# Column sums, folds and score matmuls of a hybrid decoder step: partial work moved from TensorE to VectorE, transposes for folds, page loads reordered

## What is computed

```python
(s_m, a_m, g_m, s_f, a_f, g_f) = silu(c) @ W_ada + b_ada
h = RMSNorm(x) * (1 + a_m) + s_m
p = h @ W_in
A = MLA(p)         # latent attention; the samples attend to paged cache rows
B = ShortConv(p); C = ChunkGMLP(p)
x = x + g_m * W_o(sig(gA)*A + sig(gB)*B + sig(gC)*C)
x = x + g_f * MoE(RMSNorm(x) * (1 + a_f) + s_f)    # 64 experts, top 8, 1 shared
```

## Time and profile before

| | |
|---|---|
| median of 3 runs | 1101.2 us |
| the profiled execution | 1101.79 us |
| its span (first to last instruction) | 1100.1 us |
| TensorE busy | 1052.6 us (96%) |
| VectorE busy | 387.0 us (35%) |
| ScalarE busy | 226.8 us (21%) |
| mean granted TensorE clock | 0.985 |

### The profile page before, as it was taken

One profiled execution on the slowest core, in us unless ns is written; L12 is line 12 of the kernel. 1 busy time (PEld: TensorE's weight loads), 2 busy tenths in 40 slices (PEclk: granted clock), 3 DMA queues, 4 the chain that ended last, 5 costly groups with the idle time before them and its releaser, 6 DMA issues.

```text
span 1100.1 us, 14510 instructions
## 1 busy us (share of the span) xinstructions
PE 1052.6 (96%) x4963; PEld 606.4 (55%) x4963; DVE 387.0 (35%) x1057; ACT 226.8 (21%) x464; POOL 56.6 (5%) x80
## 2 busy tenths in 40 slices
PE   7999999888999899999899999999999999999996
PEld 3477766444444678887673444444444444444443
DVE  1403211246774111112362334334334343433334
ACT  2311222133443300000421111111111111211110
POOL 0100001000000000000010000000000000000000
PEclk9999999899999999999899999999999999999998
DMA  8974467644345672343429999999999999999971
GB/s 318 420 310 165 162 216 226 146 127 132 96 122 190 211 330 115 138 169 130 176 94 396 415 414 409 408 416 402 406 409 412 398 404 414 410 405 414 400 310 41
DMA packets 52353, 310.11 MB, mean 282 GB/s; under 512 B 8538, under 2 KB 27018, under 8 KB 30802
## 3 DMA queue, kind: packets, MB, share of 16 engines
q1 hardware_dynamic: 46018, 296.13, 69.1%
q0 software_dynamic: 6288, 13.37, 3.4%
HBM read 314.80 MB, written 2.80 MB: 289 GB/s over the span
## 4 chain that ended last, share of the span: by engine, by line
PE 86%; SPq 6%; DMA 3%; issue 3%; DVE 1%; ACT 0%; DVEq 0%; ACTq 0%
PE bank L632 48%; PE pA L632 22%; PE pB L632 6%; PE pC L632 5%; SPq L386 3%; PE bank L1153 3%; SPq L427 2%; PE bank L1143 1%; DMA adx<-in_w_ada 1%; DMA pT<-in_poolT 1%; PE bank L1173 1%; PE pD L632 0%; DVE pT L2059 0%; SPq L422 0%; PE bank L1064 0%
## 5 line engine op out<-in xcount | busy, mean ns | idle before, releaser
L632 PE MATMUL pA<-ring,qT 128*64 128x512 f32 x1024 | 226.7, 595 | 0.0
L632 PE MATMUL bank<-hT,ring 128*128 128x264 f32 (+1 forms) x864 | 199.3, 390 | 1.0 <-PE bank L632 1.0
L632 PEld LDWEIGHTS bank<-hT,ring 128*128 128x128 f32 (+1 forms) x864 | 162.9, 190 | 36.2 <-issue 8.0
L632 PEld LDWEIGHTS pA<-ring,qT 128*64 128x64 f32 x1024 | 70.8, 137 | 133.7 <-issue 133.7
L632 PE MATMUL bank<-pT,vtok 128*128 128x264 f32 x512 | 127.6, 393 | 0.9 <-ACT vtok L1561 0.9
L632 PEld LDWEIGHTS bank<-pT,vtok 128*128 128x128 f32 x512 | 92.2, 190 | 39.4 <-issue 26.9
L2059 DVE TENSOR_TENSOR pT<-pT,bank 128x264 f32<-128x264 f32 x256 | 106.8, 427 | 12.2 <-PE bank L632 9.9
L632 PE MATMUL bank<-wuk,ring 128*128 128x512 f32 x192 | 89.9, 618 | 0.0
L2067 DVE TENSOR_TENSOR oaT<-oaT,pA 128x256 f32<-128x256 f32 x32 | 13.5, 421 | 197.9 <-ACT oaT L1557 197.9
L632 PEld LDWEIGHTS bank<-wuk,ring 128*128 128x128 f32 x192 | 36.4, 197 | 47.9 <-issue 47.7
L632 PE MATMUL pB<-ring,oaT 128*64 128x512 f32 x256 | 62.0, 605 | 0.5 <-ACT oaT L1540 0.5
(11 more groups left out here) (279 smaller groups left out, 884.3 us busy)
## 6 DMA issues: line engine op xcount, KB each, us to landing
ring<-in_w_e_gu SPq DMA_DIRECT2D x64, 2048.0 KB, 10.0
ring<-in_w_e_dn SPq DMA_DIRECT2D x64, 1024.0 KB, 10.4
ring<-in_poolT SPq DMA_DIRECT2D x64, 208.0 KB, 2.7
ring<-in_w_ada SPq DMA_DIRECT2D x12, 1024.0 KB, 8.2
ring<-in_w_bg SPq DMA_DIRECT2D x4, 3072.0 KB, 10.6
ring<-in_w_mix SPq DMA_DIRECT2D x5, 2048.0 KB, 8.8
ring<-in_w_ada SPq DMA_DIRECT2D x4, 2048.0 KB, 13.2
ring<-in_poolR SPq DMA_DIRECT2D x50, 128.0 KB, 2.1
```

Of the source, the lines that this page charges most:

```text
L632: return nc.tensor.matmul(out, lhsT, rhs, start=start, stop=stop)
```

## The change

- `sumsq` becomes `colsum`: VectorE adds the tiles first (`tile_sums`, one strided TENSOR_REDUCE), and one ones-matmul adds over the partitions. This holds for norm1, cqn, kvn, vmean and vvar. In norm2 VectorE adds the squares tile by tile, and two ones-matmuls stand after the last output tile.
- `ada_fold` and `scores_fold` become four transposes against `ident`. VectorE adds over the groups (`ada_sum`, twelve of them, and a second instruction in `take_scores`). pA holds one item at a time, so a fold waits for the sum before it (`adsum`, `folded`).
- The rotary part of `scores` is four matmuls of 256 columns in four column groups.
- `qlat` is eight matmuls of 256 columns in four column groups, a copy on ScalarE and four transposes.
- On SP, `ada_item(10)` goes ahead of `pages_t(0, 1)`. 28 row pages of the second group are issued inside the sequence loop, up to five behind each `pages_t`, into space whose weights have been used; the last four follow `row_values(0)`, ahead of g0.
- On the POOL queue `ident` is loaded first, in place of `fold`; `fold2` goes.
- On VectorE the norm of the queries (`head_norm(0)`) comes ahead of `head_var("ksum", 1)`.

The diff, cut to its core:

```diff
         rowpg = [rest(0, PGE, 11) + rest(1, PGE, 11) + rest(3, H * KL + 8 * P, 10),
-                 rest(1, PGE, 11) + rest(2, QT * H * P + KT_ * H * NOPE, 7)
-                 + [qTf[:, x * KL:(x + 1) * KL] for x in range(8)] + [kTf[:, x * KL:(x + 1) * KL] for x in range(6)]]
+                 rest(2, 0, 12) + rest(2, DT * 512, 8) + [adx[:].rearrange("p a c -> p (a c)")[:, x * KL:(x + 1) * KL]
+                                                          for x in range(8)] + rest(1, PGE, 4)]
+        LATE = 4
...
             ada_item(9)
+            ada_item(10)
             pages_t(0, 1)
-            ada_item(10)
             ada_item(11)
...
-            with sp.Fori(1, NS // 2) as i:
+            for i in range(1, NS // 2):
                 for b in range(2):
                     pages_t(i, b)
+                    x = (2 * (i - 1) + b) * 5
+                    pages_r(1, x, min(x + 5, HALF - LATE))
...
             values_done(0)
+            pages_r(1, HALF - LATE, HALF)
             gates_w(0)
-            pages_r(1, 0, 18)
             gates_w(1)
-            sp.wait_ge(s["asc"], H)
-            pages_r(1, 18, HALF)
...
-            def sumsq(stage, src, nt, ready=None):
+            def colsum(stage, src, i):
                 n = BASE[stage]
                 t = enter(n)
-                for k in range(nt):
-                    last = mm(t[:, 0:NT], ones[:], src[:, k, :], k == 0, k == nt - 1)
-                last.then_inc(full[n % 4], 1)
+                pe.wait_ge(s["tilesum"], i)
+                mm(t[:, 0:NT], ones[:], src, True, True).then_inc(full[n % 4], 1)
...
             def ada_fold(x):
+                if x:
+                    pe.wait_ge(s["adsum"], x)
                 for m in range(4):
-                    last = mm(pA[:, (4 * x + m) * NC:(4 * x + m + 1) * NC], adb[:, x % 2, m * P:(m + 1) * P], fold[:],
-                              True, True)
+                    last = nc.tensor.transpose(pA[:, m * P:(m + 1) * P], adb[:, x % 2, m * P:(m + 1) * P], ident[:])
...
+            for hf in range(2):
+                for j in range(4):
+                    h = 4 * hf + j
+                    last = mm(t[32 * j:32 * j + NS, hf * KL:(hf + 1) * KL], qsg[0:NOPE, h, :], wukT[:, h, :], True, True)
+            last.then_inc(full[n % 4], 1)
+            keys(0, range(NPK // 2, NPK - 1))
...
+                    last = nc.tensor.transpose(t[:, (2 * k + hf) * P:(2 * k + hf + 1) * P],
+                                               scr[:, (2 * hf + k) * P:(2 * hf + k + 1) * P], ident[:])
...
-                for g in range(2):
-                    last = mm(t[32 * g:32 * g + 32, :], qrp[:, q, :], pgT[b][:, 4 * g:4 * g + 4, 2 * P:3 * P], False, True)
+                for k in range(KT_):
+                    for g in range(2):
+                        last = mm(t[32 * (2 * k + g):32 * (2 * k + g) + 32, k * 2 * P:(k + 1) * 2 * P], qrp[:, q, :],
+                                  pgT[b][:, 4 * g + 2 * k:4 * g + 2 * k + 2, 2 * P:3 * P], False, True)
...
                 for j in range(4):
-                    last = mm(out[:, :, j, :], scr[:, j * P:(j + 1) * P], fold2[:].rearrange("p (g h) -> p g h", g=2),
-                              True, True)
+                    last = nc.tensor.transpose(pA[:, j * P:(j + 1) * P], scr[:, j * P:(j + 1) * P], ident[:])
...
-                if m >= 2:
-                    norm2(m - 2)
-            norm2(DT - 2)
-            norm2(DT - 1)
+            pe.wait_ge(s["tilesum"], 6)
+            mm(pB[:, 0:NT], ones[:], sq[:, 0, :], True, False)
+            pe.wait_ge(s["sq2"], DT)
+            mm(pB[:, 0:NT], ones[:], sq[:, DT - 1, :], False, True).then_inc(s["norm2"], 1)
...
+            def tile_sums(out, src):
+                link(V.tensor_reduce(out=out, in_=src.rearrange("p k t -> p t k"), op=ALU.add, axis=AX.X))
+                dve.sem_inc(s["tilesum"], 1)
...
+            def ada_sum(x):
+                dve.wait_ge(s["ada_mm"], x + 1)
+                link(V.tensor_reduce(out=adf[:, 4 * x:4 * x + 4], in_=pA[:].rearrange("p (m j c) -> p m c j", m=4, j=4)
+                                     [:, :, 0:NC, :], op=ALU.add, axis=AX.X))
+                dve.sem_inc(s["adsum"], 1)
...
-            early_sums(0, 6)
+            early_sums(0, 4)
+            dve.wait_ge(s["sq1"], 1)
+            tile_sums(rstd[:], sq[:])
+            early_sums(4, 6)
```

More of the change, by code:

```diff
@@ L744, in _ @@
             mixed(1, "cb", range(4))
[L745 to L748, removed]
+            colsum("cqn", sq[:, QT + KT_, :], 2)
+            colsum("kvn", sq[:, QT + KT_ + 1, :], 3)
+            pe.wait_ge(d_late, 16 * 7)
             ada_item(4)
-            mixed(3, "cc", (0,))
+            mixed(3, "cc", range(4))
             ada_fold(4)
-            mixed(3, "cc", (1, 2, 3))
             pe.wait_ge(s["cqn"], 1)
@@ L829, in _ @@
             t = enter(n)
-            for k in range(KT_):
[L831 to L835, removed]
+            for hf in range(2):
[4 more added lines that the diff above has]
+            keys(0, range(NPK // 2, NPK - 1))
+            m = BASE["qlatT"]
+            t = enter(m)
+            pe.wait_ge(free[n % 4], n // 4 + 1)
+            for k in range(KT_):
+                for hf in range(2):
+                    last = nc.tensor.transpose(t[:, (2 * k + hf) * P:(2 * k + hf + 1) * P],
+                                               scr[:, (2 * hf + k) * P:(2 * hf + k + 1) * P], ident[:])
+            last.then_inc(full[m % 4], 1)
+            keys(0, (NPK - 1,))
             pe.wait_ge(s["qlat"], 2)
@@ L893, in gmlp @@
             def gmlp(step_):
-                n = BASE[step_]
                 if step_ == "vmean":
-                    t = enter(n)
-                    pe.wait_ge(s["in_done"], 1)
-                    for k in range(CT):
-                        last = mm(t[:, 0:NT], ones[:], pT[:, T_V + k, :], k == 0, k == CT - 1)
-                    last.then_inc(full[n % 4], 1)
+                    colsum("vmean", rstd[:], 4)
                 elif step_ == "vvar":
-                    pe.wait_ge(s["sqv"], 1)
-                    sumsq("vvar", vsq, CT)
+                    colsum("vvar", rstd[:], 5)
                 elif step_ == "vtr":
@@ L1024, in _ @@
                     through(n, 2 + hf)
-            def norm2(k):
-                pe.wait_ge(s["sq2"], k + 1)
-                last = mm(pB[:, 0:NT], ones[:], sq[:, k, :], k == 0, k == DT - 1)
-                if k == DT - 1:
-                    last.then_inc(s["norm2"], 1)
             pe.wait_ge(s["merged"], DT)
@@ L1391, in squares @@
                     act.sem_inc(free[n % 4], 1)
-            squares(0, range(NPK))
+            squares(0, range(NPK // 2))
+            n = BASE["qlat"]
+            t = fulls(n)
+            nc.scalar.activation(scr, t[:], ACT.Copy).then_inc(free[n % 4], 1)
+            squares(0, range(NPK // 2, NPK))
             def score_rows(q):
@@ L1690, in _ @@
             big = pT[:, T_CC:T_CC + H, :]
+            ada_sum(4)
             dve.wait_ge(s["qcopy"], H)
@@ L1695, in _ @@
             dve.sem_inc(s["qrot"], 1)
+            ada_sum(5)
             dve.wait_ge(s["mix_done"], 1)
```

87 lines of the change are left out of this document (53 added, 34 removed).

## The result

The changed kernel takes **1081.3 us** (median, 1077.83 to 1081.71), the kernel before in the same comparison 1100.9 us (1098.32 to 1101.7). The ratio is 0.982, with a 95% interval of 0.9805 to 0.9836. The forecast was 1079.1 us with a range of 1072 to 1088. The profiled execution took 1081.71 us with a span of 1079.9 us; against the profiled one before that is -20.1 us where the sum said -22.7. (The sum was taken off the profiled execution, 1101.8; taken off the median of 1101.2 it gives 1078.5.)

The account below looks back on a forecast made before the run. TensorE was taken as the bound (86% of the chain of waits), with SP's queue setting scores(2). Terms -11.5 (1.9 + 3.0 + 6.6) - 4.4 - 5.1 - 1.7 = -22.7 against 1101.8 gave 1079.1 us, range 1072 to 1088.

Parts of the forecast that it names:

- The opening: Up to in0: seven norm1 ones-matmuls and cheaper folds 0 to 3, against a wait for VectorE's sum; -1.9 us.
- The projections: cqn and kvn lose three ones-matmuls (-1.35) and folds 4 to 7 get cheaper (-1.7); -3.0 us.
- The entry: Entry to the sequence loop: item 11 lands earlier, low clock behind its wait goes, chunk 11 ends sooner; -6.6 us.
- The wait before scores(2): TensorE's wait for SP's pages of sequence 2 grows from 3.3 to about 11 us; scores(2) comes 11.5 us earlier.
- The loop: From scores(2) on: cheaper score folds, rotary part and vvar, less 2.6 us of low clock; -4.4 us.
- Row values: Second group: the 3.3 us wait for row pages and the low clock behind it (1.8) go; -5.1 us.
- norm2: Five ones-matmuls fewer ahead of the end of out(7) (-2.2), one more VectorE add (+0.5); -1.7 us.
- (1): Item 11 stays late, held back by the broadcast; the entry's 6.6 us go, 1085.7 us; chance 0.17.
- (2): Row pages become the loop's pace: SP slips or g0 lands late, up to 5 us lost, 1084 us; chance 0.12.
- (3): Groups and sums free: norm1's sum 2.4 us, no clock loss, no wait for item 11; 1073.4 us; chance 0.12.
- (4): Slower: the clock does not come back after the 11 us wait; 1120 to 1160 us; chance 0.03.
- (5): Waits on VectorE's semaphores eat each fold's gain; only rows and item 11 count, 1086 to 1090 us; chance 0.06.

Follow-up runs that it names:

- n1_pe: The change with norm1's column sum on TensorE again, eight ones-matmuls and no sum on VectorE; 1082.1 us.
- sum_twice: The change with norm1's strided sum on VectorE done twice; 1085.4 us.
- sp_back: The change with both orders of SP undone (item 10 behind the pages, second-group row pages as before), compute parts alone; 1090.0 us.
- ada10_back: The change with ada_item(10) behind pages_t(0, 1) again; 1083.9 us.
- rows_back: The change with the second group's row pages as before: g0, 18 pages, g1, 14 pages, outside the sequence loop; 1085.5 us.
- spread: The change with 14 first-group row pages, not 32, ahead of sequence 2's pages; later rows dealt 8, 5, 5, 5, 5, 18; 1078.6 us.
- fit_halve: As fit, with norm1's tiles added on VectorE by three contiguous additions; 1065.3 us.
- spread_halve: As spread, with norm1's tiles added on VectorE by three contiguous additions instead of one strided sum; 1080.5 us.
- fit: As spread, but 18 row pages behind chunk 11, then 6, 6, 6, 7, 6, 8, and g0 directly after row_values(0); 1069.0 us.
- before_spread: The kernel before with the SP orders of spread and no compute part; 1098.6 us.

## Why the prediction was right, and where not

The forecast of 1079.1 us missed the median by 2.2 us. The path that it named is the one that the runs show: the end of item 11 starts SP's pages, these start scores(2), and what TensorE saves in between is lost. Some of its steps were wrong in ways that the total hides, and that part is luck: the opening gave nothing, the queue after item 11 was shorter than assumed, and item 11 was issued earlier than the text said.

- **The opening, -1.9 said, -0.1 measured.** This step failed. Its price of norm1's sum was right (4.0 said, the rows below), and so was the wait (2.4 said, 2.5 measured). What it left out is the clock: behind that wait TensorE ran at 0.59 and 0.56, so that eight MATMULs took 5.13 us and not 3.67. I had counted such a loss for the long wait only. Of the -0.1, moreover, -0.4 was there before norm1, as the first pages came earlier in this execution. n1_pe and sum_twice put the price on it: eight ones-matmuls cost no more than the wait with its low clock, and further time of the sum arrives at scores(2). In the three profiles in which the clock stayed the opening is 1.7 to 2.5 us shorter than with the old text, about as forecast; so the step fails by whether the clock falls, which differs between executions. Groups of VectorE by shape, for the strided sums of eight, four, three and two tiles (L1630) and the ada sums (L1646):

```profile
L1630 DVE TENSOR_REDUCE rstd<-sq 128x264 f32<-128x2112 f32 x1 | 4.0, 3956 | 3.0 <-ACT sq L1286 3.0
L1630 DVE TENSOR_REDUCE rstd<-pT 128x264 f32<-128x1056 f32 x2 | 3.9, 1940 | 0.2
...
L1630 DVE TENSOR_REDUCE sq<-sq 128x264 f32<-128x792 f32 x1 | 1.1, 1058 | 21.7 <-ACT sq L1309 21.7
L1630 DVE TENSOR_REDUCE sq<-sq 128x264 f32<-128x528 f32 x1 | 0.7, 712 | 0.1
...
L1646 DVE TENSOR_REDUCE ada<-pA 128x36 f32<-128x144 f32 x12 | 3.7, 304 | 42.9 <-PE pA L667 42.9
```

- **The projections, -3.0 said, -3.1 measured.** cqn, kvn and four folds, as priced. Their two sums were priced too high on VectorE, where nothing waits for them: 1.06 and 0.71 us, where 1.6 and 1.1 were said.
- **The entry, -6.6 said, -6.8 measured.** The wait for item 11 (1.5 said, 1.0 measured) and the low clock behind it went as said. The attribution was too simple. "Item 11 is still issued near 185" was wrong as it stands: the issue follows the end of chunk 9 and moved with it to 181.4, for the most part by the 3.2 us that the terms ahead had already saved. The sum needs it to be wrong: it put item 11's landing on the clock time of the new kernel and TensorE's arrival on that of the old one, and then added the 1.9 and 3.0 us of the terms ahead. Issued at 185.00 and landing as measured in 11.2 us, item 11 would have let chunk 11 end at 198.3 (an estimate from these rows) and not at 194.6. And the order of item 10 is not the whole of it: sp_back, without it, landed in 14.3 us, and the order's own worth is 2.6 us (the change against ada10_back) to 4.4 us (rows_back against sp_back). The profiles together show the order more plainly than the pairs of times: with item 10 behind the pages item 11 took 13.8 to 15.8 us to land (three profiles), with it ahead 10.7 to 12.8 in ten profiles and 16.0 in one. How long it takes differs from one execution to the next, so that a finer split stays open.
- **The wait before scores(2), "about 11 us": 10.2.** Here one term was missing that hid the miss of the opening: the 32 rows and 8 pages went from 205.45 to 250.10 before, 44.7 us, and from 195.42 to 238.74 after, 43.3 us. scores(2) came 11.4 us earlier where 11.5 were said, and that agreement is luck. SP's loop over the pages is unrolled in the change, which is the likely cause: from the end of chunk 11 to scores(2) it is 48.2 us before and 46.8 to 47.5 in the seven profiles with the unrolled loop and 32 rows ahead. No run undoes the unrolling alone.
- **The loop, -4.4 said, -3.9 measured.** The groups of TensorE behind two of its terms answer to the earlier trace rows:

```profile
L632 PE MATMUL bank<-ring,pT 128*32 128x256 f32 x64 | 5.4, 411 | 0.0
L868 PE MATMUL pA<-ident,pT 128*128 128x128 f32 x32 | 5.2, 286 | 0.7 <-ACT pT L1397 0.7
```

  From its start to the next instruction's, the rotary part takes 0.55 us and 0.96 before, -0.41 where -0.45 was said. A score fold takes 0.49 and 0.91 before, so -0.42 and not -0.51: the old fold's 1.06 had a tail that runs beside the next matmul, which I had taken off for the ones-matmuls and not here. The low clock behind the long wait cost 2.9 us (9.64 us for 28 MATMULs that take 6.78 in later turns), 2.6 said. The turns from the second on are 0.8 to 0.95 us shorter, about what the two terms add up to.
- **Row values, -5.1 said, -5.0 measured.** From -15.3 at the gates to -20.3 at the latent output. rows_back brings back 4.2 us.
- **norm2, -1.7 said, -1.4 measured,** with the wait of 1.7 us at L1992.
- **The tail,** +1.2 us in the profiled execution, was in no term. From the router to the end of the span the profiled executions spread from 560.4 to 561.8 us in the ten kernels with the compute parts and from 559.1 to 561.2 in the four without. The two overlap, so that it need not be the change's; that it isn't is not shown.

**The rivals.** (1), item 11 stays late, is out: it landed at 192.5. (2), row pages as the loop's pace, is out for the change (no page wait behind scores(2)), but spread showed the mechanism with other numbers: g0 9.2 us late. (3) was right on one point, a wait for item 11 of 1.0 us. (4) is out: the clock was at 0.50 for five microseconds, at 0.70 for two, and at 1.00 from 248 to 340, with the four transposes of each of the six folds there. (5) is out: the folds wait 0.3 us in all for `adsum`.

The price of 1.8 ns for each strided element fits the sum of eight tiles: 3.96 us strided, 2.4 us for the same additions done contiguously in three instructions. It doesn't fit the sums of three and two tiles, whose elements also lie 264 apart: with the fixed 0.15 us of the prediction's working, 1058 and 712 ns are about 1.1 ns an element, near the contiguous price (1.05 ns, an estimate from the earlier trace rows), against 1.8 for eight tiles and 1.7 for four. What sets the price between three and four tiles stays open.

## What to carry to other kernels

Before pricing saved work, ask which queue sets the next start: here 10 us of TensorE time lay in a wait for SyncE's queue, and dealing its transfers by the turn in which each is read gave 12 us more without touching the arithmetic. When one resource is relieved, count what the same queue now holds back next, as g0 in spread. A partial sum moved to another engine must be ready when the matmul engine arrives: here eight tiles added contiguously took 2.4 us and not 3.96, and the wait was 0.2 us and not 2.5. Count a wait with the slower clock that may follow it: behind those 2.5 us eight MATMULs took 5.13 us and not 3.67.

## What the runs showed of the hardware

- **The clock behind short waits.** At norm1's matmul the waits of 0.2, 1.0, 1.7, 1.85 and 2.0 us (fit_halve, spread_halve, ada10_back, rows_back, spread) had full clock behind them (1.00 to 29 us, and the next ten MATMULs in 4.13 us), those of 2.5, 2.7, 2.7 and 6.7 us (the change, fit, sp_back, sum_twice) half clock (down to 0.56, 0.50, 0.50 and 0.50, and the ten MATMULs in 5.83 to 6.00 us). At item 11, though, 2.7 and 3.2 us (n1_pe, ada10_back) had full clock behind them (16 MATMULs in 1.96 us), and 4.1, 4.2 and 5.8 us (sp_back, before, spread_halve) half (3.6 to 3.7 us); and 1.0 us had full clock in the change and half in before_spread, whose 16 MATMULs took 3.6 us and not 1.96. The timeline of TensorE in before_spread, and its window behind the wait:

```profile
196.49 1.07 PE L639 MATMUL bank<-ring,csig 128*32 128x512 f32 x2 [0.97 <-DMA adx<-in_w_ada]
```

```profile
197.00:198.00 1.00, 1.00 (x8) 0.23 (x4) 0.91 (x1) 0.00 (x0) 0.00 (x0) 0.50 0.76 225
```

  In the kernel before, 3.3 us ahead of scores(2) had full clock behind them (1.00 from 253 to 260), and 3.3 us ahead of the second row values half (0.50 from 378 to 380, 0.77 to 382). So the same length of wait goes either way, in different places and in the same place. The length of the wait at norm1 goes with how the first pages arrive: in the executions with half clock TensorE had waited 0.3 to 0.5 us for them, in those with full clock 0.6 to 1.5.
- **How long the half clock lasts.** Behind the 10.2 us wait before scores(2) it held for 5.8 us in the change, behind 10.3 us in rows_back for 2.7 us, with the same instructions following: the first 28 MATMULs took 9.64 us in the one and 8.14 in the other. Both are single profiles; what sets the length is not shown.
- **A strided sum from PSUM at the contiguous price.** `ada_sum` reads 144 elements, with 32 between those that it adds, in 304 ns, where I had expected 0.4 us by the strided price of SBUF; with a fixed 0.15 us that is 1.07 ns an element, the contiguous price. As the sums of two and three tiles in SBUF cost no more, this is not shown to be PSUM's doing.
- **A transfer of one size has no one price.** The adx half of item 11, 1 MB, took 10.7 to 16.0 us from issue to landing in the fourteen profiled kernels.
- **How the work shows.** The time is 1.7 to 1.9 us above the span in every run of all fourteen kernels. The one ones-matmul of norm1 shows as two MATMULs, the four transposes of a fold as four. TensorE's instructions overlap: the 32 transposes of L868 have a mean of 286 ns each, 9.2 us together, and their busy time is 5.2 us.
